# Two couples of time mixing on one core: the output product in two parts, and another order of steps, readers and banks

## The reference, cut to what matters

```python
def rwkv7_scan(r, decay, k, v, kk, a):
    # S_t = S_{t-1} (diag(w_t) - kk_t^T (a_t * kk_t)) + v_t^T k_t ;  y_t = S_t r_t
    def step(state, inp):
        r_t, w_t, k_t, v_t, kk_t, a_t = inp
        sa = jnp.einsum("bhvk,bhk->bhv", state, -kk_t)
        state = (state * w_t[:, :, None, :] + sa[..., None] * (kk_t * a_t)[:, :, None, :]
                 + v_t[..., None] * k_t[:, :, None, :])
        y = jnp.einsum("bhvk,bhk->bhv", state, r_t)
        return state, y
...
    y = rwkv7_scan(rh, wh, kh, vh, kk, ah)
    mean = jnp.mean(y, -1, keepdims=True)
    var = jnp.mean(jnp.square(y - mean), -1, keepdims=True)
    y = ((y - mean) * lax.rsqrt(var + GN_EPS)).reshape(B, S, RWKV_WIDTH)
    y = y * lnx_w + lnx_b
    bonus = jnp.sum(rh * kh * r_k, -1, keepdims=True) * vh
    y = y + bonus.reshape(B, S, RWKV_WIDTH)
    return (y * g).astype(p.dtype)
```

## Time and profile before

| | us |
|---|---|
| median of 3 runs | 1938.46 |
| lowest, highest | 1937.6, 1938.72 |
| the profiled execution | 1938.3 |
| its span, first to last instruction | 1936.5 |

### The profile page before, as it was taken

How to read it: one execution, slowest core, us unless ns; L and a number is a source line. 1 busy time by engine, 2 the same in 40 slices (tenths; PEclk the granted TensorE clock), 3 DMA queues, 4 the chain that set the end, 5 groups by cost and what they waited for, 6 DMA issues and landing times.

```text
span 1936.5 us, 31701 instructions
## 1 busy us (share of the span) xinstructions
PE 1910.5 (99%) x13490; PEld 1644.9 (85%) x13490; DVE 1333.3 (69%) x1755; ACT 837.4 (43%) x1254; POOL 120.8 (6%) x130
## 2 busy tenths in 40 slices
PE   8999999999999999999999999999999999999998
PEld 6877897888788898887989889889887788898897
DVE  5576859576677777667545687767677768777665
ACT  4243744354354344344224453434444645334342
POOL 1155100000000000010000000000002300000000
PEclk9999999999999999999999999999999999999999
DMA  8221402237123233224220232323342113233231
GB/s 271 88 65 66 137 9 84 83 132 130 44 90 106 89 109 109 88 81 139 88 87 23 66 101 95 109 87 110 106 140 87 50 49 104 91 106 109 87 109 44
DMA packets 138827, 182.55 MB, mean 94 GB/s; under 512 B 4917, under 2 KB 103429, under 8 KB 138304
## 3 DMA queue, kind: packets, MB, share of 16 engines
q1 hardware_dynamic: 135392, 168.91, 26.8%
q0 software_dynamic: 3296, 11.63, 2.9%
HBM read 172.66 MB, written 7.34 MB: 93 GB/s over the span
## 4 chain that ended last, share of the span: by engine, by line
PE 95%; DVE 3%; ACT 1%; issue 1%; DMA 0%; SPq 0%; DVEq 0%; ACTq 0%
PE X L1653 20%; PE M L1565 19%; PE M L1566 19%; PE M L1567 19%; PE X L687 2%; PE M L1626 1%; PE M L1628 1%; PE M L1627 1%; PE M L1981 1%; PE X L1958 1%; PE X L1969 1%; PE X L1836 1%; PE X L1805 1%; PE M L674 0%; DVE w_lo L2455 0%
## 5 line engine op out<-in xcount | busy, mean ns | idle before, releaser
L1566 PE MATMUL M<-u,raw_lo 128*128 128x512 f32 x728 | 287.9, 396 | 0.0
L1565 PE MATMUL M<-u,w_hi 128*128 128x512 f32 x728 | 287.9, 395 | 0.0
L1567 PE MATMUL M<-u,w_hi 128*128 128x512 f32 x728 | 286.1, 393 | 0.0
L2077 ACT ACTIVATE w_hi<-raw 128x2048 fp32r<-128x2048 f32 x113 | 215.6, 1908 | 91.2 <-PE M L1567 47.9
L2132 ACT ACTIVATE us<-X 128x256 f32<-128x256 f32 x156 | 60.0, 385 | 427.1 <-PE X L1653 427.1
L2605 DVE TENSOR_TENSOR h<-h,M 128x512 f32<-128x512 f32 x184 | 123.6, 684 | 144.9 <-PE M L1567 144.8
L1653 PE MATMUL X<-t,w_hi 128*128 128x256 f32 x936 | 173.2, 282 | 0.0
L1567 PEld LDWEIGHTS M<-u,w_hi 128*128 128x128 f32 x728 | 137.7, 189 | 32.9
L1565 PEld LDWEIGHTS M<-u,w_hi 128*128 128x128 f32 x728 | 136.8, 188 | 30.8
L1566 PEld LDWEIGHTS M<-u,raw_lo 128*128 128x128 f32 x728 | 136.7, 188 | 29.7
L2455 DVE TENSOR_TENSOR raw_lo<-raw,w_hi 128x2048 fp32r<-128x2048 f32 x57 | 130.3, 2286 | 23.7 <-ACT w_hi L2077 23.7
(11 more groups left out here) (509 smaller groups left out, 4527.9 us busy)
## 6 DMA issues: line engine op xcount, KB each, us to landing
raw<-in_w_up_dram SPq DMA_DIRECT2D x48, 1024.0 KB, 5.3
raw<-in_w_down_dram SPq DMA_DIRECT2D x48, 1024.0 KB, 5.0
raw<-in_w_in_dram SPq DMA_DIRECT2D x12, 1024.0 KB, 7.8
raw<-in_a_w_in_dram SPq DMA_DIRECT2D x12, 1024.0 KB, 5.4
h<-in_x_dram SPq DMA_DIRECT2D x16, 256.0 KB, 4.4
raw<-in_w_mk_dram SPq DMA_DIRECT2D x4, 1024.0 KB, 4.9
raw<-in_w_mv_dram SPq DMA_DIRECT2D x4, 1024.0 KB, 5.2
raw<-in_w_out_dram SPq DMA_DIRECT2D x4, 1024.0 KB, 5.3
```

The costliest lines, as they stand in the source:

```text
L1565: mm(dst, wh, xh, start=start, stop=False)
L1566: mm(dst, wl, xh, start=False, stop=False)
L1567: return mm(dst, wh, xl, start=False, stop=stop)
L2077: nc.scalar.activation(hi_of(n)[:, :, :], raw[:, n % 4], ACT.Copy).then_inc(S["w_hi_ready"], 1)
```

## The change

`Y` becomes two operations. `YA` is the first half (it owns the banks and is followed by no wait), `Y` the second half, with the banks of `YA` and a wait for the count that `YA` raises; `rw_half` and `half_done` go. Readers of the banks are looked up for `YA` (VectorE's `var`, as before). The lists are reordered and banks renumbered:

```diff
-RW_QUAD = ("L", "RBT", "AR", "PQ", "WG", "MR", "N", "Y")
+RW_QUAD = ("L", "RBT", "AR", "PQ", "WG", "MR", "N", "YA")
...
 RW_PE
-    TT6.0.1 Z2.1.2 X.1.3 WG.0.2 TT6.1.0 MR.0.1 WG.1.2 N.0.0 fill.25 S1.0.0 MR.1.1 S2.0.1 N.1.2 S3.0.0 S1.1.1 S4.0.0 S2.1.1
-    fill.26 S5.0.0 S3.1.1 fill.27 S6.0.0 S4.1.1 kk2.3.2 S5.1.0 Y.0.2 S6.1.0
-    Y.1.0 var.0.2 var.1.3 fill.28 tV.2.2 fill.29 fill.30 bonus.2.2 fill.31 gate.0.3 gate.1.0 fill.32 tV.3.1 fill.33 fill.34
-    tKd.2.1 L.2.2 fill.35 tBd.2.1 fill.36 RBT.2.1 P2.2.1 PT2.2.0 AR.2.2 P4.2.1 PQ.2.1 L.3.2 TT3.2.0 P8.2.1
-    tA.2.2 fill.37 tBd.3.0 bonus.3.3 tA.3.0 fill.38 tKd.3.0 fill.39 TT4.2.0 P2.3.1 PT2.3.2 Z.2.0 RBT.3.2 P4.3.1 PQ.3.1
+    TT6.0.1 Z2.1.2 X.1.3 WG.0.2 TT6.1.0 MR.0.1 WG.1.2 N.0.0 MR.1.1 N.1.2 S1.0.0 fill.25 S2.0.0 S1.1.1 fill.26 S3.0.0 S2.1.1
+    fill.27 S4.0.0 S3.1.1 YA.0.2 S5.0.0 S4.1.1 YA.1.1 S6.0.0 S5.1.1 fill.28 S6.1.1 Y.0.2 Y.1.1
+    var.0.1 kk2.3.0 var.1.1 tV.2.1 fill.29 fill.30 bonus.2.4 fill.31 gate.0.0 gate.1.1 fill.32 tV.3.3 fill.33 fill.34
+    tKd.2.3 L.2.2 fill.35 tBd.2.3 fill.36 RBT.2.1 P2.2.1 PT2.2.0 AR.2.2 P4.2.1 PQ.2.1 L.3.2 P8.2.1
+    tA.2.0 TT3.2.2 fill.37 tBd.3.0 bonus.3.3 tA.3.0 fill.38 tKd.3.0 fill.39 TT4.2.0 P2.3.1 PT2.3.2 Z.2.0 RBT.3.2 P4.3.1 PQ.3.1
...
-    MR.2.1 WG.3.2 N.2.0 fill.41 S1.2.0 MR.3.1 S2.2.1 N.3.2 S3.2.0 S1.3.1 S4.2.0 S2.3.1 fill.42 S5.2.0 S3.3.1
-    S6.2.0 S4.3.1 fill.43 S5.3.0 Y.2.1 S6.3.0 fill.44 var.2.0 fill.45 Y.3.0 gate.2.2 var.3.3 fill.46 fill.47 gate.3.2
+    MR.2.1 WG.3.2 N.2.0 MR.3.1 N.3.2 S1.2.0 fill.41 S2.2.0 S1.3.1 fill.42 S3.2.0 S2.3.1 YA.2.2 S4.2.0 S3.3.1
+    YA.3.1 S5.2.0 S4.3.1 fill.43 S6.2.0 S5.3.1 fill.44 S6.3.1 Y.2.2 Y.3.1 var.2.0 fill.45 gate.2.1 var.3.0 fill.46 fill.47 gate.3.1
 RW_ACT
-    PT4.1 P8.0 P8.1 sq.3 Z.0 Z.1 Z2.0 X.0 yd.0 Z2.1 tA.1 X.1 W.0 G.0 W.1 N.0 G.1 yd.1 yd.2 N.1 yd.3 w.7 dsq.0 ln.3 dsq.1 rn.3
-    var.0 grs.0 tV.2 var.1 ex.3 neg.2 grs.1 ex.2 inc.2 inc.3 dc.3 tV.3 dec.2 dc.2 tKd.2 neg.3 w.8 tBd.2 dec.3 P2.2 PT2.2 P4.2
+    PT4.1 P8.0 P8.1 sq.3 Z.0 Z.1 Z2.0 X.0 yd.0 Z2.1 tA.1 X.1 W.0 G.0 W.1 G.1 N.0 N.1 yd.1 yd.2 yd.3 w.7 dsq.0 dsq.1 ln.3 rn.3
+    var.0 grs.0 var.1 tV.2 ex.3 neg.2 grs.1 ex.2 inc.2 inc.3 dc.3 tV.3 dec.2 dc.2 tKd.2 neg.3 w.8 tBd.2 dec.3 P2.2 PT2.2 P4.2
...
-    PT4.2 P8.2 tA.2 tBd.3 tA.3 yr.0 tKd.3 w.9 P2.3 PT2.3 Z.2 P4.3 PT4.3 yr.1 P8.3 Z2.2 X.3 Z.3 X.2 Z2.3 W.2 G.2 W.3 N.2 G.3 N.3
-    dsq.2 var.2 grs.2 dsq.3 var.3 yr.2 grs.3 w.10 yr.3""".split()
+    PT4.2 P8.2 tA.2 tBd.3 tA.3 yr.0 tKd.3 w.9 P2.3 PT2.3 Z.2 P4.3 PT4.3 yr.1 P8.3 Z2.2 X.3 Z.3 X.2 Z2.3 W.2 G.2 W.3 G.3 N.2 N.3
+    dsq.2 dsq.3 var.2 grs.2 var.3 yr.2 grs.3 w.10 yr.3""".split()
 RW_DVE
-    TT6.1 MT.0 RT.0 yd.0 S1.0 S2.0 MT.1 S3.0 RT.1 S1.1 S4.0 S2.1 S5.0 yd.1 S3.1 S6.0 yd.2 S4.1 S5.1 S6.1 w.7 kk2.3 t.2 ev.12
+    TT6.1 MT.0 RT.0 yd.0 MT.1 S1.0 RT.1 S2.0 S1.1 S3.0 S2.1 ev.12 S4.0 S3.1 S5.0 S4.1 S6.0 S5.1 yd.1 S6.1 w.7 yd.2 kk2.3 t.2
...
-    K.2 ev.15 B.2 kmod.3 Kd.2 ev.16 R.2 yc.1 bonus.2 Bd.2 L.2 PT.2 gate.1 RBT.2 A.3 B.3 K.3 RKT.2 Kd.3 rk.3 AKT.2 TT2.2 ev.17
-    Bd.3 TT3.2 L.3 R.3 w.8 PT.3 TT4.2 T4.2 ev.18 ev.19 RBT.3 bonus.3 TT2.3 yr.0 TT5.2 T5.2 TT3.3 AKT.3 TT4.3 TT6.2 T4.3 RKT.3
-    TT5.3 T5.3 TT6.3 MT.2 RT.2 S1.2 S2.2 MT.3 S3.2 RT.3 S1.3 S4.2 S2.3 S5.2 S3.3 S6.2 S4.3 w.9 ev.20 S5.3 S6.3 var.2 yb.2 yc.2
+    K.2 ev.15 B.2 kmod.3 Kd.2 ev.16 bonus.2 R.2 yc.1 Bd.2 L.2 PT.2 gate.1 RBT.2 A.3 B.3 K.3 RKT.2 AKT.2 Kd.3 rk.3 TT2.2 ev.17
+    Bd.3 TT3.2 L.3 R.3 w.8 PT.3 TT4.2 T4.2 bonus.3 ev.18 ev.19 RBT.3 TT2.3 yr.0 TT5.2 T5.2 TT3.3 AKT.3 TT4.3 TT6.2 T4.3 RKT.3
+    TT5.3 T5.3 TT6.3 MT.2 RT.2 MT.3 S1.2 RT.3 S2.2 S1.3 S3.2 S2.3 S4.2 S3.3 S5.2 S4.3 S6.2 S5.3 w.9 ev.20 S6.3 var.2 yb.2 yc.2
...
-        RW_BANKS[_x] = RW_QUAD_SETS[_b] if _x[0] in RW_QUAD else (_b,)
+        RW_BANKS[_x] = RW_BANKS[("YA", _x[1])] if _x[0] == "Y" else RW_QUAD_SETS[_b] if _x[0] in RW_QUAD else (_b,)
...
-    if st == "Y":
+    if st == "YA":
         return [("d", ("var", hp))]
...
-                         S1=["a.N", "d.MT"], Y=["d.S6", "d.RT", "d.RKT", "a.G"], gate=[], var=["a.dsq"])
+                         S1=["a.N", "d.MT"], YA=["d.RKT", "a.G"], Y=["d.S6", "d.RT"], gate=[], var=["a.dsq"])
...
-                    half_done(last)
+                else:
+                    wait("rw_mm", RW_NO["p"][("YA", hp)])
                     for c in range(1, 8):
```

More of the change, by code:

```diff
@@ L177 @@
+    tA.2.0 TT3.2.2 fill.37 tBd.3.0 bonus.3.3 tA.3.0 fill.38 tKd.3.0 fill.39 TT4.2.0 P2.3.1 PT2.3.2 Z.2.0 RBT.3.2 P4.3.1 PQ.3.1
     TT5.2.0 P8.3.1 TT3.3.2 Z2.2.0 AR.3.2 TT4.3.1 TT6.2.0 X.3.2 Z.3.1 X.2.3 TT5.3.1 fill.40 Z2.3.1 WG.2.2 TT6.3.0
-    MR.2.1 WG.3.2 N.2.0 fill.41 S1.2.0 MR.3.1 S2.2.1 N.3.2 S3.2.0 S1.3.1 S4.2.0 S2.3.1 fill.42 S5.2.0 S3.3.1
-    S6.2.0 S4.3.1 fill.43 S5.3.0 Y.2.1 S6.3.0 fill.44 var.2.0 fill.45 Y.3.0 gate.2.2 var.3.3 fill.46 fill.47 gate.3.2""".split()
+    MR.2.1 WG.3.2 N.2.0 MR.3.1 N.3.2 S1.2.0 fill.41 S2.2.0 S1.3.1 fill.42 S3.2.0 S2.3.1 YA.2.2 S4.2.0 S3.3.1
@@ L180 @@
+    YA.3.1 S5.2.0 S4.3.1 fill.43 S6.2.0 S5.3.1 fill.44 S6.3.1 Y.2.2 Y.3.1 var.2.0 fill.45 gate.2.1 var.3.0 fill.46 fill.47 gate.3.1""".split()
 RW_ACT = """zw.0 za.0 sq3.0 zw.1 w.2 za.1 zw.2 za.2 zw.3 za.3 sq.0 dn.0 w.3 dec.0 sq.1 ln.0 rn.0 dc.0 neg.0 w.4 dc.1 dec.1 inc.0 ex.0 tKd.0
     ex.1 ln.1 rn.1 sq.2 tV.0 neg.1 inc.1 tBd.0 tV.1 tKd.1 w.5 tBd.1 PT2.0 tA.0 P2.0 PT2.1 P2.1 w.6 P4.0 PT4.0 ln.2 rn.2 P4.1
-    PT4.1 P8.0 P8.1 sq.3 Z.0 Z.1 Z2.0 X.0 yd.0 Z2.1 tA.1 X.1 W.0 G.0 W.1 N.0 G.1 yd.1 yd.2 N.1 yd.3 w.7 dsq.0 ln.3 dsq.1 rn.3
@@ L228, in rw_users @@
     for x in RW_OPS["p"]:
-        if x[0] != "fill":
+        if x[0] == "Y":
+            after[x] = []
+        elif x[0] != "fill":
             after[x] = sorted({user[b] for b in RW_BANKS[x] if b in user})
@@ L252, in program @@
             da_sq da_ss da_ln da_rstd da_y
-            rw_shift rw_p rw_lora rw_act rw_dve rw_half rw_mm y_hi y_lo
+            rw_shift rw_p rw_lora rw_act rw_dve rw_mm y_hi y_lo
             ms_hi ms_lo ma_score ma_max ma_neg ma_exp ma_rz ma_p ma_tr ma_pt_hi ma_pt_lo ma_pv ma_hi ma_lo
@@ L601, in operand @@
                 return blk(sl(name, hp), hh, cp, cpar)
[L603 to L609, removed]
             def out_of_psum(st, hp):
@@ L692, in rwkv_pe @@
                                   start=True, stop=True)
-                elif st != "Y":
+                elif st == "N":
                     for cp in range(4):
@@ L700, in rwkv_pe @@
                                 last = mm(o_, tmv(2, hp, hh, cp, cpar), tmv(3, hp, hh, cp, cpar), start=False, stop=True)
-                else:
+                elif st == "YA":
                     for cp in range(4):
```

## The result

| | us |
|---|---|
| changed kernel, median of 7 runs | 1945.7 (1943.12 to 1946.18) |
| kernel before, beside it | 1938.68 |
| ratio | 1.0034, 95% interval 1.0022 to 1.0046 |
| the profiled execution | 1945.08, span 1943.2, mean granted clock 0.996 |

Slower by 0.34%, outside my range of 1935.6 to 1940.4. By the ratio that is 6.6 us, by the two medians 7.0. The ratio leaves out one of the seven runs of the kernel before, which took 2332.8 us. The profile's code lines have moved up by 5 or 6; `S` steps are L685 now, `var` L637 (TensorE) and L1019 (VectorE), `tV` L640, fills of 128x512 L1560 to L1562, `ev` L2473, `w_lo` L2450, VectorE's `kk2` L930, `bonus` L943, ScalarE's operations L744.

What follows compares the result with a forecast made beforehand. TensorE, busy 1910.5 of 1936.5 us, was taken as the bound. It would enter the output projection 0.6 early, less 0.1 for couple 1: 1938.46 - 0.5 = 1938.0 us, range 1935.6 to 1940.4.

Steps and rivals of the forecast that it cites:

- The first recurrence: State steps of couples 0 and 1: removed waits sum to 2.1 us; `var.0` starts at 291.2, before at 293.30.
- The stretch up to `N.2`: Middle of time mixing, couples 2 and 3: TensorE becomes 0.6 us early and stays so to `N.2`.
- `var.1` waits 2.8: Behind the first recurrence: `var.1` shares bank 1 with `var.0` and waits 2.8 us for ScalarE's read.
- `tV.2` 0.9: After `var.1`: `tV.2` has bank 1 too and waits 0.9 us for ScalarE's read of `var.1`.
- `kk2.3` on VectorE at 293.5: Behind `var.0`: VectorE's half of `kk2.3` begins at 293.5 us, for 292.56 before.
- `L.2` waits 0.5: Couple 2: `L.2` needs bank 4 and waits 0.5 us until VectorE has read `bonus.2`.
- `P8.2` starts "within 0.1": Couple 2: `P8.2`, issued before `TT3.2`, starts where `TT3.2` started before, within 0.1 us.
- `PQ.3` keeps 0.5: Couple 3: `PQ.3` waits only for `RBT.3`, so 0.5 of its 1.1 us wait stays.
- The recurrence of couples 2 and 3: Second state recurrence and its tail: removed waits make TensorE another 1.6 us early, of which nothing is left.
- 0.8 of it comes back as a wait: Second recurrence: `Y.3` waits 0.8 us for `S6.3`, behind `w.9` and `ev.20` on VectorE.
- rival B: Pause at `var.1`: the clock falls there, costing 1.8 us, total 1939.8; chance 0.15.
- the 1.8 of the start: Start of the span: 3.7 us, 8.3 to 12, read as at the lower clock level, losing half, 1.8 us.

Runs made afterwards that it cites:

- e8: Changed kernel with matmuls that nobody reads filling both long TensorE pauses, ahead of `var.1` and ahead of `fill.44`; 1940.41 us.
- e9: Changed kernel with matmuls that nobody reads only in the first pause, ahead of `var.1`; 1942.58 us.
- e1: Changed kernel with ScalarE reading `var.0` (and `grs.0`) before `ln.3` and `rn.3`; 1942.61 us.
- e2: Changed kernel with `ev.20` and `S6.3` ahead of the weight split `w.9` on VectorE; 1940.79 us.
- e5: Changed kernel with ScalarE reading `var.0` first and, on VectorE, `w.9` behind `S6.3`, `ev.20` behind `S2.3`, `ev.21` right behind `S6.3`; 1937.39 us.
- e4: Changed kernel with half fill `fill.28` moved from before `S6.1` to between `kk2.3` and `var.1` on TensorE; 1942.1 us.

## Why the prediction was wrong

Right were the parts that rest on chains of named operations:
- The first recurrence: `var.0` at 291.2, measured 291.45. All waits listed as removed there are gone.
- The stretch up to `N.2`: 0.6 early, measured 0.3 to 0.5 early where the clock stayed up (e8, e9, e1).
- `var.1` waits 2.8, measured 2.77; `tV.2` 0.9, measured 0.78; `kk2.3` on VectorE at 293.5, measured 293.47.
- `L.2` waits 0.5: measured 0.21 with TensorE already late, 0.5 in the kernels whose clock did not fall in the first pause. `P8.2` starts "within 0.1" of `TT3.2`'s place: it waits 0.3 for `PT4.2`, a small miss. `PQ.3` keeps 0.5: measured 0.59.

Wrong were two steps.

**The recurrence of couples 2 and 3.** "0.8 of it comes back as a wait", at `Y.3` for `S6.3` behind `w.9`. I saw `w.9` in the way and asked only which state step stands behind it. But `ev.20` stands behind it too, and `fill.44`, which the change moved from behind `S6.3` to ahead of it, needs `ev.20`. I had costed the moved fills at 1.6 each and taken their banks for free, though `bank_free` in the fill says that they are not. Measured 3.14 for 0.8, and 0.98 at `fill.46` for `ev.21`, which I had not either. With the clock held up (e8), the kernel is 1.7 slower where I had 0.5 faster, 2.2 us apart; nearly all of it lies from `N.2` to `gate.3`, 26.43 us for 24.47 before, where my sum had no change. e2, which moves `w.9` alone, brings 4.9, and e5 another 1.6 by the `ev` that the fills wait for.

**The clock.** I had it as rival B, with a chance of 0.15 and a price of 1.8 for one fall, and "the sum takes nothing for it". Measured: it falls in both pauses and costs 5.3 by the medians, some 3 each. The price was mis-sized since I took the 1.8 of the start, 3.7 us at the lower level, where the first fall lasts 6.8; it begins in the pause and goes on behind it through `var.1`, its second wait, `tV.2` and a fill, for which VectorE then waits (1.36 us, up to 303.35). The reading of the start itself was sound: in the changed kernel 128x512 matmuls at a granted clock of 0.50 take the same 0.63 (378.11), although the clock column of the profile says 1.00 from 8 to 12. The Trainium skill ("TensorE: Matmul & The Clock Gate", What's actually happening) says that throttled is the default state and that activity releases it. The trace agrees as far as it goes: 0.50 after a pause, 1.00 again when TensorE has been at work. The second fall hangs on the pause that I had not seen. And the sign that a short pause can be enough stood in the trace of the kernel before, between the two slices of the earlier trace rows that I used:

```profile
1930.00:1931.00 1.00, 0.00 (x0) 0.00 (x0) 0.55 (x2) 0.42 (x1) 0.00 (x0) 0.70 0.00 0
```

TensorE's last work ended at 1929.46, and the clock fell at about 1930.4, less than 1 us later, behind a wait of 1.4 and 0.7 us of work. I had written that no row tells between 0.9 and 8.3 us, and gave the fall a chance of 0.15.

The range was too narrow because all cases in it had the missed wait in common, and because of B's price: with some 3 us for one fall, 1938.0 + 3 would already have been above it.

## What to carry to other kernels

Where work of another stream is used to fill gaps, a filler has a bank and a reader of its own: when it is moved, follow the reader in its engine's list, and see what long instruction stands before it. In a schedule that keeps TensorE full, price a new pause twice, once for its idle time and once for the clock: here the clock cost more than the idle time (some 3 us for each of two pauses of 2.8 and 3.1 us by the medians, 1 to 2.5 in single profiles), and the idle time of one pause cost next to nothing. Look at the granted clock in slices of 1 us before looking for anything else. Of a reordering with many parts, undo single tokens: one VectorE instruction moved by two places was worth 4.9 us here, ten times the 0.5 that I forecast for the whole change.

## What the runs showed of the hardware

- A fall of the clock needs no single long pause: in e4 it fell to 0.50 behind 1.36 us of idle time, 1.1 us of work and half of another 0.78, while 1.7 us of idle time (e1, at `tV.2`) and in the same run 3.14 us did not bring it down. The same order of work brought a fall of 6.8 us at 295.7 (changed kernel) and one of 3.4 us at 298.4 (e2). No run here separates what decides it.
- With the pauses filled by matmuls that nobody reads, the clock stayed at 1.00: thirteen of them, some 6 us of TensorE time (2.75 and 3.29 in e8's profile), made the kernel 5.3 us faster by the medians.
- At the lower level two 128x512 float32 passes took 2.08 us for 1.02 at the upper one (L637 at 296.21 against the earlier trace rows).
